# Retention scores and value products as three float32r passes, at later places of a head's pass

## The chip, the cores and the metric

One core of one Trainium2 chip runs the whole kernel. The metric is the device time of one execution in microseconds (us); the median of several runs is compared.

## The reference

The kernel computes one block of a diffusion backbone for 256 latent and 256 context tokens of width 2048 in float32. The latent tokens go through `w_in`, then two attention-like branches of four heads each (retention and gated linear attention, GLA), which are merged by gates, and then a SwiGLU network. What the change touches is the retention branch, for each head:

```python
q_r = apply_rope(to_heads(rq, RET_HEADS), cos, sin) * (RET_DK ** -0.5)
k_r = apply_rope(to_heads(rk, RET_HEADS), cos, sin)
o_r = bidirectional_recurrence(q_r, k_r, v, la_f, la_b, kc, vc, lac_f, lac_b)   # heads of 256 wide
o_r = merge_heads(head_layer_norm(o_r)) * ret_gn * silu(rg)
```

With one decay per head the recurrence is `o = ((q k^T) * decay) v` over 512 keys: 256 of the context, without rope, and 256 latent.

## The kernel before, in words

**Large products.** Every product with a weight matrix is done in float32r, in three passes: the float32 operand is split into a high part (a copy rounded to float32r) and a low part (the value less the high part), and high x high, low x high and high x low are added up in PSUM. A weight slot is 256 rows by 512 columns. SP loads it into `raw` (8 buffers), ScalarE's `split` copies it to `w_hi` (L648), VectorE's `split` subtracts to `w_lo` (L1055), and TensorE's `products` (L1639, L1643, L1651) uses both. `w_hi` and `w_lo` have 4 buffers (`SPLIT`), so ScalarE may split slot p only once TensorE has used slot p - 4 (`w_used`).

**Heads.** The projection `h @ w_in` runs for 15 latent blocks of 8 slots. The heads of both branches are spread over it: one head takes a pass of 16 slots, and `head_pass` calls `at_head(i, p)` behind the slot with number p - 4 of head i's pass, so that the small steps of a head stand between slots on TensorE's queue. ScalarE and VectorE carry out their steps with the same p ahead of their own split of slot p. Each engine's order is written out by hand and each engine takes its queue in order; steps wait for each other by semaphores. Between passes, steps 0 to 3 of the next head stand behind slots 12 to 15.

The steps of a head that matter here, with TensorE's place p before the change:

- p = 3: r_kc transposed into bank 4; ScalarE (p = 4) copies it to `r_kt[:, 0:2]`.
- p = 6: rotated r_q and r_k transposed into banks 5 and 4 (L1907); ScalarE (p = 6) copies them to `r_qt` and `r_kt[:, 2:4]` (L865, L867), then takes the Exp of the far GLA levels (`level_exp`, L834) and only then splits slot 6.
- p = 7: the scores (L1925), fp32, 8 matmuls. VectorE (p = 7, behind its split of slot 6) multiplies the level exponentials (`weigh`, L1268).
- p = 8: the far levels of the GLA (L1891, L1897), which need `weigh`. VectorE (p = 8) weights the scores by the decay into `r_a` (L1329).
- p = 9: the value products (L1941), fp32, 8 matmuls into bank 4.
- p = 10: the GLA values (L1916 to L1919), which need `g_a`. VectorE's `pick_far` (p = 10, behind its split of slot 9) copies bank 6 and parts of `g_near` into `g_a` (L1289, L1294). VectorE then takes the statistics of the retention output (L1337 to L1343), and at p = 11 those of the GLA output.
- p = 13 and 14: the normalised and gated outputs r_g (L1948) and g_g (L1933) transposed; VectorE prepares them at p = 12 and 13 and moves the results to `o_t` at p = 14 and 15.

GpSimd rotates r_q and r_k (`head`, L533 to L537), takes the roots of the variances (L550, L554), and issues the loads of the next head's q, k, v and gates from DRAM (L498). At p of 12 and more, VectorE also takes the near exponents of the next head; at p = 5 the far ones (L1234 to L1237).

## Time and profile before

| | |
|---|---|
| Median of 3 runs | 1721.49 us (1719.5 to 1721.71) |
| The profiled execution's own time | 1720.11 us |
| Its span, first to last instruction | 1718.4 us |
| TensorE busy | 1692.7 us |
| VectorE, ScalarE, GpSimd busy | 1008.8, 740.4, 164.3 us |
| HBM read | 397.99 MB, 244 GB/s over the span with the writes |

The profile is of one execution. A matmul's record includes the time in which its result runs out of the array, so records of a dense stream overlap, and the distance of their starts is what one costs. A fp32 matmul leaves two records, a float32r matmul one. PEld are the weight loads. In the timeline, neighbouring instructions of one kind are merged (xN), and in brackets stands how long the engine idled before, and what released it. Where rows name a line, it is that of the kernel before.

### The profile page before, as it was taken

The page shows a single profiled execution, that of the slowest core. Times are in us where ns is not written, and L with a number is a line of the kernel's source. Part 1 is how long each engine was busy: PE and PEld are TensorE (multiplying, and loading weights), DVE is VectorE, ACT ScalarE, POOL GpSimd, SP SyncE. Part 2 cuts the span into 40 slices and gives each one's busy share as a digit, 9 for nine tenths or more (in the row PEclk, how much of TensorE's full clock was granted, in tenths as well). Part 3 has the DMA queues.
Part 4 walks back from the last instruction along what each step waited for, and adds up shares of the span by engine and source line. Part 5 has one row for each costly group of instructions (what it writes and reads, how often), then busy time and mean ns, then how long its engine had stood idle before and what let it go on. Part 6 is the DMA issues. An engine that isn't in the chain of part 4 may idle for free.

```text
span 1718.4 us, 21875 instructions
## 1 busy us (share of the span) xinstructions
PE 1692.7 (99%) x8109; PEld 1363.7 (79%) x8109; DVE 1008.8 (59%) x1146; ACT 740.4 (43%) x832; POOL 164.3 (10%) x179
## 2 busy tenths in 40 slices
PE   6999999999999999999999999999999999999998
PEld 2458888887878888888888788888888888888886
DVE  2446767748966777666665764454545454444444
ACT  3324222217555454445446654444444444443442
POOL 0011000000046355220000000000000000000000
PEclk9999999999999999999999999999999999999999
DMA  9999999978988666656776566666666666766662
GB/s 366 377 381 372 353 343 363 347 279 304 374 302 275 197 220 197 212 148 222 227 263 218 183 224 192 186 193 185 191 187 189 189 188 189 262 193 193 195 193 90
DMA packets 183676, 419.35 MB, mean 244 GB/s; under 512 B 12960, under 2 KB 13328, under 8 KB 173760
## 3 DMA queue, kind: packets, MB, share of 16 engines
q1 hardware_dynamic: 167680, 375.45, 66.4%
q0 software_dynamic: 7184, 27.71, 4.9%
q10 hardware_dynamic: 8752, 15.38, 2.4%
q8 instruction: 39, 0.64, 0.2%
q14 instruction: 21, 0.17, 0.0%
HBM read 397.99 MB, written 20.50 MB: 244 GB/s over the span
## 4 chain that ended last, share of the span: by engine, by line
PE 96%; DVE 2%; DMA 1%; issue 1%; ACT 0%; POOL 0%; SPq 0%; DVEq 0%; POOLq 0%; ACTq 0%
PE ps L1639 28%; PE ps L1643 28%; PE ps L1651 28%; PE ps L1721 2%; PE ps L1695 2%; DMA raw<-in_w_mod 1%; PE ps L1737 1%; PE ps L1941 1%; PE ps L1925 1%; PE ps L1979 1%; PE ps L1866 0%; PE ps L1684 0%; DVE xr_t L424 0%; PE ps L2057 0%; PE ps L2044 0%
## 5 line engine op out<-in xcount | busy, mean ns | idle before, releaser
L1055 DVE TENSOR_TENSOR w_lo<-raw,w_hi 128x1024 fp32r<-128x1024 f32 x486 | 602.6, 1243 | 501.2 <-ACT w_hi L648 500.9
L648 ACT ACTIVATE w_hi<-raw 128x1024 fp32r<-128x1024 f32 x488 | 515.7, 1060 | 774.0 <-PE ps L1651 758.7
L1639 PE MATMUL ps<-w_hi,h_hi 128*128 128x512 f32 x1440 | 452.6, 395 | 0.0
L1643 PE MATMUL ps<-w_hi,h_lo 128*128 128x512 f32 x1440 | 445.3, 389 | 0.0
L1651 PE MATMUL ps<-w_lo,h_hi 128*128 128x512 f32 x1440 | 392.4, 389 | 0.0
L1643 PEld LDWEIGHTS ps<-w_hi,h_lo 128*128 128x128 f32 x1440 | 270.3, 188 | 56.8
L1651 PEld LDWEIGHTS ps<-w_lo,h_hi 128*128 128x128 f32 x1440 | 270.2, 188 | 56.4
L1639 PEld LDWEIGHTS ps<-w_hi,h_hi 128*128 128x128 f32 x1440 | 266.8, 188 | 55.6 <-ACT w_hi L648 1.5
L1067 DVE SCALAR_TENSOR_TENSOR acc<-wm,csil,acc 128x2048 f32<-128x2048 f32 x60 | 141.0, 2350 | 60.9 <-DMA wm<-in_w_mod 60.8
L1639 PE MATMUL ps<-w_hi,hid_hi 128*128 128x512 f32 x352 | 109.8, 389 | 0.0
L1643 PE MATMUL ps<-w_hi,hid_lo 128*128 128x512 f32 x352 | 109.7, 389 | 0.0
L1651 PE MATMUL ps<-w_lo,hid_hi 128*128 128x512 f32 x352 | 94.7, 389 | 0.0
L1643 PEld LDWEIGHTS ps<-w_hi,hid_lo 128*128 128x128 f32 x352 | 66.1, 188 | 13.8
L1651 PEld LDWEIGHTS ps<-w_lo,hid_hi 128*128 128x128 f32 x352 | 66.1, 188 | 13.7
L1639 PEld LDWEIGHTS ps<-w_hi,hid_hi 128*128 128x128 f32 x352 | 66.0, 188 | 13.7
L1643 PE MATMUL ps<-w_hi,hc_lo 128*128 128x512 f32 x192 | 59.1, 389 | 0.0
L1639 PE MATMUL ps<-w_hi,hc_hi 128*128 128x512 f32 x192 | 59.1, 389 | 0.0
L1651 PE MATMUL ps<-w_lo,hc_hi 128*128 128x512 f32 x192 | 57.8, 389 | 0.0
L1695 PE MATMUL ps<-raw,c_pad 128*32 128x512 f32 x256 | 46.3, 631 | 7.7 <-DMA raw<-in_w_mod 5.8
L628 POOL DMA_DIRECT2D hs<-hsd x1 | 0.7, 718 | 479.2 <-DVE hid_n L1585 479.2
L1117 DVE TENSOR_TENSOR w_lo<-raw,w_hi 128x1024 fp32r<-128x1024 f32 x16 | 19.3, 1223 | 44.5 <-ACT w_hi L721 44.5
L1643 PEld LDWEIGHTS ps<-w_hi,hc_lo 128*128 128x128 f32 x192 | 36.0, 188 | 7.5
(315 smaller groups left out, 1390.5 us busy)
## 6 DMA issues: line engine op xcount, KB each, us to landing
raw<-in_w_in SPq DMA_DIRECT2D x184, 512.0 KB, 6.5
wm<-in_w_mod SPq DMA_DIRECT2D x64, 1024.0 KB, 7.1
raw<-in_ffn_w_gate SPq DMA_DIRECT2D x88, 512.0 KB, 4.4
raw<-in_ffn_w_up SPq DMA_DIRECT2D x88, 512.0 KB, 4.4
raw<-in_ffn_w_down SPq DMA_DIRECT2D x88, 512.0 KB, 4.6
raw<-in_w_mod SPq DMA_DIRECT2D x64, 512.0 KB, 8.1
raw<-in_w_out SPq DMA_DIRECT2D x32, 512.0 KB, 4.8
px<-stage ACTq DMA_DIRECT2D x44, 256.0 KB, 6.1
```

Source lines behind the costliest of these rows:

```text
L648: act.activation(w_hi[:, j % SPLIT, :, :], raw[:, j % RAW, :, :], ACT.Copy).then_inc(w_high, 1)
L1055: dve.tensor_tensor(w_lo[:, j % SPLIT, :, :], raw[:, j % RAW, :, :], w_hi[:, j % SPLIT, :, :].bitcast(F32), ALU.subtract).then_inc(w_low, 1)
L1067: dve.scalar_tensor_tensor(out=a, in0=wm[:, b, :], scalar=csil[:, k:k + 1], in1=a, op0=ALU.mult, op1=ALU.add).then_inc(S("wm_used"), 1)
L1117: dve.tensor_tensor(w_lo[:, o % SPLIT, :, :], raw[:, place % RAW, :, :], w_hi[:, o % SPLIT, :, :].bitcast(F32), ALU.subtract)\
L1639: pe.matmul(o, hi[:, kk, c], w_h[:, e, :], start=kk == 0, stop=False)
L1643: pe.matmul(o, lo[:, kk, c], w_h[:, e, :], start=False, stop=False)
L1651: last = pe.matmul(o, hi[:, kk, c], w_l[:, e, :], start=False, stop=kk == last_k)
L1695: last = pe.matmul(bank(6)[g * GROUP:(g + 1) * GROUP, :], c_pad[:, k, :], raw[:, place % RAW, e, :], start=k < 4, stop=k >= KT - 4, tile_p ...
L1721: last = pe.matmul(bank(n), t[:, 2 * i + e, m * P:(m + 1) * P], w[:, q, e, :], start=i == 0 and r == 0 and a == 0, stop=i == 7 and r == 2 ...
L1737: last = pe.matmul(bank(4 + m), t[:, 2 * i + e, m * P:(m + 1) * P], w[:, q, e, :], start=i == 0 and a == 0, stop=i == 7 and a == 5)
L1925: last = pe.matmul(bank(4, 2)[:, a * L:(a + 1) * L], r_kt[:, 2 * (a // 2) + f, (a % 2) * P:(a % 2 + 1) * P], r_qt[:, f, :], start=f == 0, ...
L1941: last = pe.matmul(bank(4)[:, m * RDK:(m + 1) * RDK], r_a[:, a, m * P:(m + 1) * P], r_v[:, a, :], start=a == 0, stop=a == 3)
```

## The change

- Scores: `r_qt` and `r_kt` become float32r high parts; VectorE makes `r_kt_lo` (context half at p = 4, latent half at p = 7) and `r_qt_lo` (p = 7, ahead of `weigh`). TensorE's scores are 24 float32r matmuls and move from p = 7 to p = 8, ahead of the far levels. The low parts lie in the place of r_q, r_k and r_kc.
- Value products: ScalarE makes `r_v_hi` (p = 7) and `r_a_hi` (p = 10), VectorE `r_v_lo` (p = 8) and `r_a_lo` (p = 10, behind `pick_far`). `r_a` itself moves from p = 8 to p = 9 on VectorE. TensorE's value products are 24 float32r matmuls and move from p = 9 to p = 11. The low part of v lies in v's place, that of a in a's place, `r_a_hi` in the place of the rope's products, `r_v_hi` in that of `ctx_w1`.
- The retention statistics move from VectorE's p = 10 to p = 12; the two branches change places at p = 12 to 15 on VectorE and at p = 13 and 14 on TensorE.
- GpSimd issues the next head's r_kc, r_q and r_k with the v loads, behind `r_o_done` and `g_o_done`; the two roots and the two gate loads change places.

```diff
@@ -179,8 +180,14 @@
 r_v = reg("r_v", [P, 4, RDK], 6)
 r_g = reg("r_g", [P, MT, RDK], 10)
 r_tmp = reg("r_tmp", [P, 4, MT, P], 12)
-r_qt = reg("r_qt", [P, 2, L], 16)
-r_kt = reg("r_kt", [P, 4, L], 18)
+r_qt = reg("r_qt", [P, 2, L], 16, F32R)
+r_kt = reg("r_kt", [P, 4, L], 18, F32R)
+r_qt_lo = reg("r_qt_lo", [P, 2, L], 0, F32R)
+r_kt_lo = reg("r_kt_lo", [P, 4, L], 2, F32R)
+r_v_hi = at("r_v_hi", [P, 4, RDK], F32R, ctx_w1_off)
+r_v_lo = reg("r_v_lo", [P, 4, RDK], 6, F32R)
+r_a_hi = reg("r_a_hi", [P, 4, L], 12, F32R)
+r_a_lo = reg("r_a_lo", [P, 4, L], 22, F32R)
 r_a = reg("r_a", [P, 4, L], 22)
 g_q = reg("g_q", [P, MT, GDK], 26)
 g_k = reg("g_k", [P, MT, GDK], 27)
@@ -542,28 +549,26 @@
         load_g_qk(i + 1)
         pool.wait_ge(S("g_state_done"), i + 1)
         load_g_kw(i + 1)
-        pool.wait_ge(S("r_kc_turned"), i + 1)
-        load_r_kc(i + 1)
-        pool.wait_ge(S("r_qk_turned"), i + 1)
-        load_r_qk(i + 1)
+    pool.wait_ge(S("g_ms_ready"), i + 1)
+    pool.tensor_tensor(hr[:, 1, :, :], mv[:, 1, :, 0:1],
+                       minus_half[:, 0:MT].rearrange("p (m o) -> p m o", o=1), ALU.pow)\
+        .then_inc(S("g_rstd_ready"), 1)
     pool.wait_ge(S("r_var_ready"), i + 1)
     pool.tensor_tensor(hr[:, 0, :, :], mv[:, 0, :, 1:2],
                        minus_half[:, 0:MT].rearrange("p (m o) -> p m o", o=1), ALU.pow)\
         .then_inc(S("r_rstd_ready"), 1)
-    pool.wait_ge(S("g_ms_ready"), i + 1)
-    pool.tensor_tensor(hr[:, 1, :, :], mv[:, 1, :, 0:1],
-                       minus_half[:, 0:MT].rearrange("p (m o) -> p m o", o=1), ALU.pow)\
-        .then_inc(S("g_rstd_ready"), 1)
     if not last:
         pool.wait_ge(S("r_o_done"), i + 1)
         pool.wait_ge(S("g_o_done"), i + 1)
+        load_r_qk(i + 1)
+        load_r_kc(i + 1)
         load_v(i + 1)
-        pool.wait_ge(S("r_on_turned"), i + 1)
-        load_r_gate(i + 1)
         pool.wait_ge(S("g_on_turned"), i + 1)
         pool.wait_ge(stored[0], 16 * 11)
         pool.wait_ge(stored[1], 16 * 11)
         load_g_gate(i + 1)
+        pool.wait_ge(S("r_on_turned"), i + 1)
+        load_r_gate(i + 1)
...
@@ -859,19 +864,24 @@
         if p == 4:
             act.wait_ge(S("r_kc_turned"), i + 1)
             act.activation(r_kt[:, 0:2, :], bank(4).rearrange("p (f n) -> p f n", f=2), ACT.Copy)\
-                .then_inc(S("r_kct_ready"), 1)
+                .then_inc(S("r_high"), 1)
         if p == 6:
             act.wait_ge(S("r_qk_turned"), i + 1)
             act.activation(r_qt[:, :, :], bank(5).rearrange("p (f n) -> p f n", f=2), ACT.Copy,
-                           scale=RDK ** -0.5).then_inc(S("r_qkt_ready"), 1)
+                           scale=RDK ** -0.5).then_inc(S("r_high"), 1)
             act.activation(r_kt[:, 2:4, :], bank(4).rearrange("p (f n) -> p f n", f=2), ACT.Copy)\
-                .then_inc(S("r_qkt_ready"), 1)
+                .then_inc(S("r_high"), 1)
             level_exp(i, 1)
+        if p == 7:
+            act.wait_ge(S("r_v_landed"), i * 32 + 32)
+            act.activation(r_v_hi[:, :, :], r_v[:, :, :], ACT.Copy).then_inc(S("r_high"), 1)
         if p == 9:
             act.wait_ge(S("g_levels_done"), i * 2 + 2)
             act.activation(g_a[:, 2:4, :], bank(7)[:, L:2 * L].rearrange("p (a n) -> p a n", a=2), ACT.Copy)\
                 .then_inc(S("g_cross_ready"), 1)
         if p == 10:
+            act.wait_ge(S("r_a_ready"), i + 1)
+            act.activation(r_a_hi[:, :, :], r_a[:, :, :], ACT.Copy).then_inc(S("r_high"), 1)
             act.wait_ge(S("gates_landed"), i * 32 + 32)
             act.activation(g_g[:, :, :], g_g[:, :, :], ACT.Silu).then_inc(S("g_silu"), 1)
             act.activation(r_g[:, :, :], r_g[:, :, :], ACT.Silu).then_inc(S("r_silu"), 1)
@@ -1322,26 +1332,32 @@
             pick_near(i)
             for e in range(4):
                 exponents(i, 4 + e)
+        if p == 4:
+            dve.wait_ge(S("r_high"), i * 5 + 1)
+            dve.tensor_tensor(r_kt_lo[:, 2:4, :], bank(4).rearrange("p (f n) -> p f n", f=2),
+                              r_kt[:, 0:2, :].bitcast(F32), ALU.subtract).then_inc(S("r_low"), 1)
         if p == 7:
+            dve.wait_ge(S("r_high"), i * 5 + 3)
+            dve.scalar_tensor_tensor(out=r_qt_lo[:, :, :], in0=bank(5).rearrange("p (f n) -> p f n", f=2),
+                                     scalar=RDK ** -0.5, in1=r_qt[:, :, :].bitcast(F32),
+                                     op0=ALU.mult, op1=ALU.subtract).then_inc(S("r_low"), 1)
+            dve.tensor_tensor(r_kt_lo[:, 0:2, :], bank(4).rearrange("p (f n) -> p f n", f=2),
+                              r_kt[:, 2:4, :].bitcast(F32), ALU.subtract).then_inc(S("r_low"), 1)
             weigh(i, 1)
         if p == 8:
+            dve.wait_ge(S("r_high"), i * 5 + 4)
+            dve.tensor_tensor(r_v_lo[:, :, :], r_v[:, :, :], r_v_hi[:, :, :].bitcast(F32), ALU.subtract)\
+                .then_inc(S("r_low"), 1)
+        if p == 9:
             dve.wait_ge(S("r_scores_done"), i + 1)
             dve.tensor_tensor(r_a[:, :, :], bank(4, 2).rearrange("p (a n) -> p a n", a=4),
                               dmat[:, bass.ds(i, 1), :, :].rearrange("p o a n -> p (o a) n"), ALU.mult)\
                 .then_inc(S("r_a_ready"), 1)
         if p == 10:
             pick_far(i)
-
-            dve.wait_ge(S("r_o_done"), i + 1)
...
+            dve.wait_ge(S("r_high"), i * 5 + 5)
+            dve.tensor_tensor(r_a_lo[:, :, :], r_a[:, :, :], r_a_hi[:, :, :].bitcast(F32), ALU.subtract)\
+                .then_inc(S("r_low"), 1)
         if p == 11:
             dve.wait_ge(S("g_o_done"), i + 1)
             for m in range(MT):
@@ -1358,6 +1374,24 @@
                                      in1=mv[:, 1, :, 1:2], op0=ALU.add, op1=ALU.add)\
                 .then_inc(S("g_ms_ready"), 1)
         if p == 12:
+            dve.wait_ge(S("r_o_done"), i + 1)
+            for m in range(MT):
+                dve.bn_stats(stats[:, 0, m, :], bank(4)[:, m * RDK:(m + 1) * RDK]).then_inc(S("r_stat"), 1)
+            dve.wait_ge(S("r_stat"), i * 4 + 2)
+            hold(8)
+            for m in range(MT):
+                dve.bn_aggr(mv[:, 0, m, :], stats[:, 0, m, :]).then_inc(S("r_stat"), 1)
+            dve.wait_ge(S("r_stat"), i * 4 + 4)
+            dve.tensor_scalar(mv[:, 0, :, 1:2], mv[:, 0, :, 1:2], EPS, None, ALU.add)\
+                .then_inc(S("r_var_ready"), 1)
+            dve.wait_ge(S("g_rstd_ready"), i + 1)
+            dve.wait_ge(S("g_silu"), i + 1)
+            for m in range(MT):
+                last = dve.scalar_tensor_tensor(out=g_g[:, m, :], in0=bank(6)[:, m * GDV:(m + 1) * GDV],
+                                                scalar=hr[:, 1, m, :], in1=g_g[:, m, :],
+                                                op0=ALU.mult, op1=ALU.mult)
+            last.then_inc(S("g_on_ready"), 1)
+        if p == 13:
             dve.wait_ge(S("r_silu"), i + 1)
             for m in range(MT):
                 dve.scalar_tensor_tensor(out=r_g[:, m, :], in0=bank(4)[:, m * RDK:(m + 1) * RDK],
@@ -1368,24 +1402,16 @@
             for m in range(MT):
                 last = dve.tensor_scalar(r_g[:, m, :], r_g[:, m, :], hr[:, 0, m, :], None, ALU.mult)
             last.then_inc(S("r_on_ready"), 1)
-        if p == 13:
-            dve.wait_ge(S("g_rstd_ready"), i + 1)
-            dve.wait_ge(S("g_silu"), i + 1)
...
         if p == 14:
+            dve.wait_ge(S("g_on_turned"), i + 1)
+            dve.tensor_tensor(o_t[:, 1, bass.ds(i * 2, 2), :], bank(7).rearrange("p (a n) -> p a n", a=2),
+                              cols[:, bass.ds(i * 2 + 72, 2)].rearrange("p (a o) -> p a o", o=1)
+                              .broadcast_to([P, 2, L]), ALU.mult).then_inc(S("gla_head_done"), 1)
+        if p == 15:
             dve.wait_ge(S("r_on_turned"), i + 1)
             dve.tensor_tensor(o_t[:, 0, bass.ds(i * 2, 2), :], bank(5).rearrange("p (a n) -> p a n", a=2),
                               cols[:, bass.ds(i * 2 + 64, 2)].rearrange("p (a o) -> p a o", o=1)
                               .broadcast_to([P, 2, L]), ALU.mult).then_inc(S("ret_head_done"), 1)
-        if p == 15:
-            dve.wait_ge(S("g_on_turned"), i + 1)
-            dve.tensor_tensor(o_t[:, 1, bass.ds(i * 2, 2), :], bank(7).rearrange("p (a n) -> p a n", a=2),
-                              cols[:, bass.ds(i * 2 + 72, 2)].rearrange("p (a o) -> p a o", o=1)
-                              .broadcast_to([P, 2, L]), ALU.mult).then_inc(S("gla_head_done"), 1)
         if p >= 12 and not final:
             exponents(i + 1, p - 12)
         if p == 15 and not final:
@@ -1885,6 +1911,17 @@
                                      g_arg[:, 0, e, c], start=True, stop=True, tile_position=(0, g * GROUP))
         last.then_inc(S("g_levels_done"), 1)
     if p == 8:
+        pe.wait_ge(S("r_low"), i * 5 + 3)
+        for a in range(4):
+            o = bank(4, 2)[:, a * L:(a + 1) * L]
+            c = slice((a % 2) * P, (a % 2 + 1) * P)
+            for f in range(2):
+                k_hi, k_lo = 2 * (a // 2) + f, 2 * (1 - a // 2) + f
+                pe.matmul(o, r_kt[:, k_hi, c], r_qt[:, f, :], start=f == 0, stop=False)
+                pe.matmul(o, r_kt[:, k_hi, c], r_qt_lo[:, f, :], start=False, stop=False)
+                last = pe.matmul(o, r_kt_lo[:, k_lo, c], r_qt[:, f, :], start=False, stop=f == 1)
+        last.then_inc(S("r_scores_done"), 1)
+    if p == 8:
         pe.wait_ge(S("g_qk_ready"), i * 2 + 2)
         pe.wait_ge(S("g_picked"), i * 9 + 4)
         for m in range(MT):
@@ -1900,7 +1937,7 @@
     if p == 6:
         pe.wait_ge(S("rope_ready"), i * 4 + 4)
         pe.wait_ge(S("ret_head_done"), i + 1)
-        pe.wait_ge(S("r_kct_ready"), i + 1)
+        pe.wait_ge(S("r_low"), i * 5 + 1)
         for b, t in ((5, r_q), (4, r_k)):
             for f in range(2):
                 for m in range(MT):
@@ -1918,30 +1955,24 @@
             pe.matmul(o, g_st[:, 0, c], g_s[:, 0, :], start=False, stop=False)
             last = pe.matmul(o, g_st[:, 1, c], g_s[:, 1, :], start=False, stop=True)
         last.then_inc(S("g_o_done"), 1)
-    if p == 7:
-        pe.wait_ge(S("r_qkt_ready"), i * 2 + 2)
-        for a in range(4):
-            for f in range(2):
-                last = pe.matmul(bank(4, 2)[:, a * L:(a + 1) * L],
-                                 r_kt[:, 2 * (a // 2) + f, (a % 2) * P:(a % 2 + 1) * P], r_qt[:, f, :],
-                                 start=f == 0, stop=f == 1)
-        last.then_inc(S("r_scores_done"), 1)
-    if p == 14:
+    if p == 13:
         pe.wait_ge(S("g_on_ready"), i + 1)
         for f in range(2):
             for m in range(MT):
                 last = pe.transpose(bank(7)[:, f * L + m * P:f * L + (m + 1) * P],
                                     g_g[:, m, f * P:(f + 1) * P], ident[:, :])
         last.then_inc(S("g_on_turned"), 1)
-    if p == 9:
-        pe.wait_ge(S("r_a_ready"), i + 1)
-        pe.wait_ge(S("r_v_landed"), i * 32 + 32)
+    if p == 11:
+        pe.wait_ge(S("r_low"), i * 5 + 5)
         for m in range(MT):
+            o = bank(4)[:, m * RDK:(m + 1) * RDK]
             for a in range(4):
-                last = pe.matmul(bank(4)[:, m * RDK:(m + 1) * RDK], r_a[:, a, m * P:(m + 1) * P],
-                                 r_v[:, a, :], start=a == 0, stop=a == 3)
+                c = slice(m * P, (m + 1) * P)
+                pe.matmul(o, r_a_hi[:, a, c], r_v_hi[:, a, :], start=a == 0, stop=False)
+                pe.matmul(o, r_a_hi[:, a, c], r_v_lo[:, a, :], start=False, stop=False)
+                last = pe.matmul(o, r_a_lo[:, a, c], r_v_hi[:, a, :], start=False, stop=a == 3)
         last.then_inc(S("r_o_done"), 1)
-    if p == 13:
+    if p == 14:
         pe.wait_ge(S("r_on_ready"), i + 1)
         for f in range(2):
             for m in range(MT):
```

The blocks left out are moved without a change to their lines. The definitions of the new tiles stand first.

## Rows read from the trace of the kernel before

**Rows 1.** The page: engines, and the granted clock in 40 slices

```profile
PE 1692.7 (99%) x8109; PEld 1363.7 (79%) x8109; DVE 1008.8 (59%) x1146; ACT 740.4 (43%) x832; POOL 164.3 (10%) x179
...
PEclk9999999999999999999999999999999999999999
```

**Rows 2.** Windows, head passes 2 and 4: us, busy PE, PEld, DVE, ACT, POOL, PEclk, DMA

```profile
607.70:668.60 60.90, 60.90 (x381) 50.82 (x380) 43.73 (x96) 29.59 (x35) 26.55 (x28) 1.00 0.66 204
...
729.50:790.20 60.70, 60.70 (x381) 50.75 (x380) 40.04 (x79) 29.65 (x35) 14.68 (x14) 1.00 0.53 158
```

**Rows 3.** Timeline of TensorE, one pass: start, duration, engine, line, count

```profile
631.34 3.61 PE L1925 MATMUL ps<-r_qt,r_kt 128*128 128x256 f32 x16
...
637.53 0.60 PE L1891 MATMUL ps<-g_arg 128*128 128x128 f32 x4
...
641.69 3.61 PE L1941 MATMUL ps<-r_v,r_a 128*128 128x256 f32 x16
...
647.87 0.59 PE L1916 MATMUL ps<-g_v,g_a 128*128 128x256 f32 x2
...
654.06 0.62 PE L1639 MATMUL ps<-w_hi,h_hi 128*128 128x512 f32 x2
...
656.78 0.62 PE L1639 MATMUL ps<-w_hi,h_hi 128*128 128x512 f32 x2
```

**Rows 4.** Source L1790: float32r matmuls of 256 columns, 64 weight columns

```profile
L1790 PE MATMUL ps<-h_hi,ga_hl x16: 276/276/281, 384.8 to 388.2; 128*64 128x256 f32 x16
```

**Rows 5.** Source L1925, timeline and groups of L1891: loads of 128 columns

```profile
L1925 PEld LDWEIGHTS ps<-r_qt,r_kt x64: 187/190/190, 570.2 to 756.1; 128*128 128x128 f32 x64
...
576.66 0.60 PE L1891 MATMUL ps<-g_arg 128*128 128x128 f32 x4
...
L1891 PE MATMUL ps<-g_arg 128*128 128x128 f32 x16 | 2.4, 273 | 0.0
```

**Rows 6.** Timeline, head 1: ScalarE, then VectorE, around slot 6

```profile
629.77 1.92 ACT L834 ACTIVATE g_arg<-g_arg 128x2048 f32<-128x2048 f32 x1
631.58 2.00 ACT L648 ACTIVATE w_hi<-raw 128x1024 fp32r<-128x1024 f32 x2
...
632.66 1.23 DVE L1055 TENSOR_TENSOR w_lo<-raw,w_hi 128x1024 fp32r<-128x1024 f32 x1 [3.37 <-ACT w_hi L648]
633.80 2.35 DVE L1268 TENSOR_TENSOR g_arg<-g_arg,g_qkt 128x1024 f32<-128x1024 f32 x2
```

**Rows 7.** Timeline, head 0: the same place, with TensorE's scores

```profile
569.46 1.92 ACT L834 ACTIVATE g_arg<-g_arg 128x2048 f32<-128x2048 f32 x1 [0.43 <-DVE g_arg L1237]
...
570.47 3.61 PE L1925 MATMUL ps<-r_qt,r_kt 128*128 128x256 f32 x16
...
572.35 1.23 DVE L1055 TENSOR_TENSOR w_lo<-raw,w_hi 128x1024 fp32r<-128x1024 f32 x1 [1.79 <-ACT w_hi L648]
```

**Rows 8.** Timeline, head 1: slot 5's release to the copies into g_a

```profile
641.88 1.06 ACT L648 ACTIVATE w_hi<-raw 128x1024 fp32r<-128x1024 f32 x1 [2.55 <-PE ps L1651]
...
644.11 0.42 DVE L1289 COPY g_a<-ps 128x256 f32<-128x256 f32 x1
...
644.82 0.75 DVE L1294 COPY_PREDICATED g_a<-mask,g_near 32x64 f32<-32x64 uint8 x3
```

**Rows 9.** Groups by form, VectorE, 548 to 791 us: mean ns of one

```profile
L1375 DVE SCALAR_TENSOR_TENSOR g_g<-ps,hr,g_g 128x256 f32<-128x256 f32 x8 | 3.5, 476 | 0.0
...
L1381 DVE TENSOR_TENSOR o_t<-ps,cols 128x512 f32 x3 | 2.0, 683 | 0.0
```

**Rows 10.** Timeline of GpSimd and TensorE, head 1; DMA issues, 600 to 665 us

```profile
618.10 1.72 POOL L537 TENSOR_TENSOR r_k<-r_tmp 128x256 f32<-128x256 f32 x1
...
630.13 0.72 POOL L498 DMA_DIRECT2D r_k<-px  x1
...
627.73 0.60 PE L1907 MATMUL ps<-ident,r_q 128*128 128x128 f32 x4
...
r_kc<-pc POOLq DMA_DIRECT2D x1, 256.0 KB, 6.5
```

More of the change, by code:

```diff
@@ L114, in build @@
         rope = keep("rope", [P, 2, MT, P])
+        ctx_w1_off = cursor[0]
         ctx_w1 = keep("ctx_w1", [P, GH, L])
@@ L1333, in head @@
                         pick_far(i)
-                        dve.wait_ge(S("r_o_done"), i + 1)
-                        for m in range(MT):
-                            dve.bn_stats(stats[:, 0, m, :], bank(4)[:, m * RDK:(m + 1) * RDK]).then_inc(S("r_stat"), 1)
-                        dve.wait_ge(S("r_stat"), i * 4 + 2)
-                        hold(8)
-                        for m in range(MT):
-                            dve.bn_aggr(mv[:, 0, m, :], stats[:, 0, m, :]).then_inc(S("r_stat"), 1)
-                        dve.wait_ge(S("r_stat"), i * 4 + 4)
-                        dve.tensor_scalar(mv[:, 0, :, 1:2], mv[:, 0, :, 1:2], EPS, None, ALU.add)\
-                            .then_inc(S("r_var_ready"), 1)
+                        dve.wait_ge(S("r_high"), i * 5 + 5)
+                        dve.tensor_tensor(r_a_lo[:, :, :], r_a[:, :, :], r_a_hi[:, :, :].bitcast(F32), ALU.subtract)\
+                            .then_inc(S("r_low"), 1)
                     if p == 11:
@@ L1370, in head @@
                         last.then_inc(S("r_on_ready"), 1)
-                    if p == 13:
-                        dve.wait_ge(S("g_rstd_ready"), i + 1)
-                        dve.wait_ge(S("g_silu"), i + 1)
-                        for m in range(MT):
-                            last = dve.scalar_tensor_tensor(out=g_g[:, m, :], in0=bank(6)[:, m * GDV:(m + 1) * GDV],
-                                                            scalar=hr[:, 1, m, :], in1=g_g[:, m, :],
-                                                            op0=ALU.mult, op1=ALU.mult)
-                        last.then_inc(S("g_on_ready"), 1)
-                    if p == 14:
+                    if p == 14:
+                        dve.wait_ge(S("g_on_turned"), i + 1)
[3 more added lines that the diff above has]
+                    if p == 15:
                         dve.wait_ge(S("r_on_turned"), i + 1)
```

## The prediction

> **What bounds the kernel now.** I read the page first: TensorE is busy in 1692.7 us of a span of 1718.4 us, at the full granted clock in every slice [rows 1]. So a change is worth what it takes off TensorE's queue, less every pause that it puts there. I then cut the trace into the four passes of 16 slots in which the heads run. TensorE is busy in all 60.9 us of each of the four (60.7 in the last), while VectorE has work for 44 us and ScalarE for 30 us [rows 2]: no wait on TensorE's queue ends late in this stretch, and each one has an unknown margin. The margins have to be read from the timelines. One pass on TensorE [rows 3]: a slot of weights without anything behind it takes 656.78 - 654.06 = 2.72 us. The scores begin at 631.34, one slot later the far levels of the GLA begin at 637.53, so the scores take 637.53 - 631.34 - 2.72 = 3.47 us; the value products likewise take 647.87 - 641.69 - 2.72 = 3.46 us.
>
> In what follows s3 means the end of TensorE's slot 3, and so on. Stage p stands on TensorE behind slot p - 4, on ScalarE and VectorE ahead of their split of slot p. ScalarE may split slot p once slot p - 4 is used.
>
> **The matmuls.** Removed: 8 fp32 matmuls for scores and 8 for values in each of four heads. Each shows as two records of 256 columns, 16 records or 3.46 us per block. Added in their place: 24 float32r matmuls of 256 columns per block. The kernel has such passes elsewhere: 32 of them (L1790 and L1791 in turn) run through 384.8 to 388.2 us, 30 gaps between the first and the last start of L1790, so 0.113 us each [rows 4]. Those load only 64 columns of weights, the new ones 128. Does a load of 128 columns fit under a pass of 0.107 to 0.113 us? Its record is 188 ns [rows 5], but four L1891 records with such loads take 0.60 us, of which the last is 0.27 us, so they follow each other at (0.60 - 0.27) / 3 = 0.11 us [rows 5]. I take 0.114 us a pass, 24 x 0.114 = 2.74 us a block. Lower end 24 x 0.107 = 2.6 us, upper end with the load's whole 0.188 us in sight 4.5 us; I stand near the lower end, because the L1891 row has the very load. Saved: 8 x (3.46 - 2.74) = 5.8 us.
>
> The Trainium skill (TensorE: Matmul & The Clock Gate, Part 3, The mechanism) says that LDWEIGHTS overlaps matmuls in flight only when the row group differs, and here all use all rows. The L1891 records don't agree with it at 0.11 us, and by them the sum stands as it is.
>
> **Wait one, the low parts ahead of the scores.** TensorE now needs r_kt_lo and r_qt_lo before the scores. They are moved one slot down to make up for that: they would start at s4 = 631.34 + 2.72 = 634.06. When are the low parts there? ScalarE starts the level Exp at 629.77, the split of slot 6 follows at 631.58, and VectorE can take its own split of slot 6 only at 632.66, after which it is free at 633.80 [rows 6]. Stage 7's new operations stand behind that split: a scalar_tensor_tensor of 128x512 out of PSUM, then a tensor_tensor of 128x512. The tensor_tensor row is 0.683 us; the other kind has 0.476 us for 256 columns, and 256 more cost about (1.23 - 0.683) / 2 = 0.27 us [rows 6, 9], so 0.75 us, of which about 0.09 overlaps with the next one (632.66 + 1.23 against 633.80). The low parts are complete at 633.80 + 0.66 + 0.68 = 635.14. That is 1.08 us after s4; with 0.05 us for the handover and 0.11 us for a first weight load that nothing hides (one step of the L1891 row), TensorE pauses for 1.2 us in heads 1 to 3. The levels need weigh's products, which move to 635.1 + 2.3 = 637.4; the scores end at 635.3 + 2.7 = 638.0, so that is covered.
>
> In head 0 it is worse. There the Exp waits for VectorE's exponents (569.46, 0.43 us of waiting) [rows 7]. The new r_kt_lo of stage 4 stands ahead of them on VectorE and delays them by 0.60 us (0.683 less the overlap); twice that is my upper end, for whatever slows it. Then the split that starts at 572.35 starts at 572.95, the low parts are complete at 572.95 + 1.14 + 1.34 = 575.43, and s4 is at 570.47 + 2.72 = 573.19 [rows 7]: a pause of 2.4 us. In heads 1 to 3 the Exp waits for ScalarE's own two copies, and 0.60 us on VectorE lies under them. Sum of this wait: 2.4 + 3 x 1.2 = 6.0 us.
>
> **Wait two, the GLA values.** L1916 is untouched in the diff, but the value products that stood between slot 5 and slot 6 go to behind slot 7. Its operand g_a comes from pick_far, in stage 10 on VectorE, behind split 9, and split 9 waits for slot 5 to be used. The chain from s5 = 641.69: ScalarE's split 9 starts at 641.88, pick_far at 644.11, and its last copy ends at 644.82 + 0.75 = 645.57 [rows 8], so 3.88 us after s5. So far TensorE had 3.46 + 2.72 = 6.18 us of work there. After the change it has slot 6 alone, 2.72 us. It pauses 3.88 - 2.72 = 1.16 us, with handover and first load 1.3 us, in every head: 5.2 us in all. The extra work on VectorE ahead of it (weigh until 637.4, split 7, r_v_lo and split 8 at 1.14 us each until 640.8, r_a until 642.0) ends before split 9 can start at about 643.7, so it adds nothing.
>
> **The rest costs nothing.** ScalarE's r_v_hi (1.06 us, as the split in [rows 8]) stands ahead of split 7, which TensorE takes 9 us later. r_a_hi follows split 9; r_a_lo is complete some 1.3 us after pick_far, about 5 us before s7, where the values now stand. The statistics and the scaling of g_g (two records of 0.476 us [rows 9] and some short ones, an estimate of 2 us behind the value products) have two slots, 5.4 us, before their transpose; r_g has one more slot. Without these covers each would cost its excess, at most 1 to 2 us a head. GpSimd's queue: r_q, r_k and r_kc are no longer loaded where r_k's issue stands at 630.13, but as the first three of seven loads behind the value products (about 656). Seven issues of 0.72 us take 5 us. The rope still waits for the last gate load, behind the second transpose, so it starts where it did; that transpose is 9 us behind the value products. r_k is ready at 618.10 + 1.72 = 619.8 and needed at 627.73, a cover of 7.9 us; a load took 6.5 us at the most [rows 10]. What is late next if it is exceeded is the transpose of stage 6, and that needs 8 us of delay. SP's queue has no edit and fetches w_in some slots ahead.
>
> **Sum.** -5.8 + 6.0 + 5.2 = +5.4 us against the profiled execution's own 1720.1 us (span 1718.4), so 1725.5 there. The median of the runs shown is 1.4 us above it at 1721.5, so 1726.9 us. Ends of the terms: passes 2.6 us a block -1.1 us; head 0's extra up to +0.6; handovers and first loads between nothing and double, -1.3 to +1.3 us. Own range 1724 to 1730.
>
> **Rivals.** What a measurement of this kernel can tell from no change is about 0.2%, 3.4 us.
>
> 1. Both pauses outweigh the shorter passes, as above: 1726.9, chance 0.62.
> 2. The other side: the low parts and g_a reach TensorE in time, because VectorE's order is not what holds them (ScalarE's split of slots 6 and 9 comes earlier than it did). Then only the passes count: 1721.5 - 5.8 = 1715.7. It is decided by the pauses' sum: below 5.8 - 3.4 = 2.4 us, or 0.3 us each, the kernel is faster. For it speaks that VectorE idles 3.37 us before split 6 [rows 6]; against it that what it idles for is ScalarE, whose order in stages 6 and 9 is the same after. Chance 0.12.
> 3. Only one of the two waits bites: -5.8 + 5.2 or + 6.0, 1721 to 1722. For it: each is an argument of about 1 us on timelines read to 0.1 us. Chance 0.16.
> 4. The weight load isn't hidden under so short a pass: 24 x (0.113 + 0.11) = 5.35 us a block, 8 x (5.35 - 3.46) = +15 us, with the pauses about 1748. Rows 5 speak against it. This is where the skill's sentence above would lead. Chance 0.04.
> 5. A further wait that I see as covered (normalisation, rope) costs 1 us a head more: 1731. Chance 0.06.
>
> The range of 8 in 10 goes from the covered edge of case 3 and part of case 2 to case 5: 1718.5 to 1731. Faster by over 0.2%: 0.13. Within: 0.20, from case 3 and the low edge of case 1. Slower: 0.67.
>
> **What the profile would show.** Right: 24 records a block in about 2.7 us; TensorE idle ahead of the scores, released by r_kt_lo, 2.4 us once and 1.2 us three times; TensorE idle ahead of L1916's successor, released by the copy into g_a, 1.3 us four times; passes of 60.9 + 1.0 us, and the rest of the span unchanged. Wrong: blocks above 3.4 us (case 4), no idle time on TensorE (case 2), or idle time with another releaser (case 5).

## The result

Before: median 1721.16 us over 8 runs (1719.5 to 1721.91). After: 1725.61 us over 8 runs (1725.18 to 1726.83). Ratio 1.0029, 95% interval [1.002, 1.0039]: slower by 4.5 us by the medians, 5.0 us by the ratio. 1726.9 us and +5.4 us were forecast. The profiled execution spans 1723.5 us against 1718.4, +5.1 us, and the heads begin within 0.15 us of each other (first transpose of head 0 at 546.90 us before, 546.75 after), so the difference lies in or behind the heads.

The page after, in the lines of [rows 1]: engines, and the granted clock in 40 slices.

```profile
span 1723.5 us, 22045 instructions
...
PE 1689.2 (98%) x8173; PEld 1361.5 (79%) x8173; DVE 1024.6 (59%) x1166; ACT 747.0 (43%) x840; POOL 164.9 (10%) x179
...
PEclk9999999999999999999999999999999999999999
```

TensorE is busy for 3.5 us less and the span is longer, at the same granted clock in each slice. So TensorE pauses. The waits on its queue in the stretch of the heads (waiting instruction <- what released it: us in all, times, the longest in us):

```profile
PE ps L1953 <- DVE g_a L1304: 4.2, 4, 1.1
PE ps L1920 <- DVE r_kt_lo L1344: 3.9, 4, 1.1
```

Two places, four times each, and no other in the heads. A window of 61.90 us over head 1's pass, against the first row of [rows 2]:

```profile
607.70:669.60 61.90, 59.92 (x397) 50.09 (x396) 48.06 (x100) 31.05 (x37) 26.39 (x28) 1.00 0.65 199
```

TensorE is busy for 59.92 us of it and idle for 1.98 us, where it was busy all the time before. The pass itself, from head 1's first transpose to head 2's, is 671.17 - 609.03 = 62.14 us long instead of 668.63 - 607.76 = 60.87. The timeline of TensorE in that pass, against [rows 3]:

```profile
634.38 1.07 PE L1677 MATMUL ps<-w_lo,h_hi 128*128 128x512 f32 x4
636.37 0.38 PE L1920 MATMUL ps<-r_qt,r_kt 128*128 128x256 f32 x1 [0.92 <-DVE r_kt_lo L1344]
...
639.34 0.61 PE L1928 MATMUL ps<-g_arg 128*128 128x128 f32 x4
...
643.50 0.62 PE L1665 MATMUL ps<-w_hi,h_hi 128*128 128x512 f32 x2
...
645.32 1.07 PE L1677 MATMUL ps<-w_lo,h_hi 128*128 128x512 f32 x4
647.44 0.70 PE L1953 MATMUL ps<-g_v,g_a 128*128 128x256 f32 x2 [1.05 <-DVE g_a L1304]
647.97 0.59 PE L1954 MATMUL ps<-g_v,g_a 128*128 128x256 f32 x2
...
653.76 0.28 PE L1971 MATMUL ps<-r_v_hi,r_a_hi 128*128 128x256 f32 x1
...
656.60 0.62 PE L1665 MATMUL ps<-w_hi,h_hi 128*128 128x512 f32 x2
```

A slot's last row of four L1677 records starts 0.91 us ahead of the slot's end (four steps of 0.2275 us; 642.60 + 0.91 = 643.51 in the complete view, where the next slot's first record stands at 643.50). Slot 4 ends at 634.38 + 0.91 = 635.29 and the scores begin at 636.37: 1.08 us. (The idle time in brackets, 0.92 us here, counts from the end of the last record, 0.16 us behind the slot's end; both figures are used below.) They end at 639.34, 2.97 us for 24 passes, of which 0.11 us is a first weight load with nothing over it. Slot 6 ends at 645.32 + 0.91 = 646.23, and L1953 begins at 647.44: 1.21 us; its second pair stands 0.53 us behind it where 0.43 us is the undisturbed distance, so another 0.10 us. The value products take 656.60 - 653.76 = 2.84 us.

What releases the scores, on ScalarE and VectorE, against [rows 6]:

```profile
631.00 1.92 ACT L839 ACTIVATE g_arg<-g_arg 128x2048 f32<-128x2048 f32 x1
...
632.81 1.06 ACT L653 ACTIVATE w_hi<-raw 128x1024 fp32r<-128x1024 f32 x1
...
633.90 1.22 DVE L1065 TENSOR_TENSOR w_lo<-raw,w_hi 128x1024 fp32r<-128x1024 f32 x1 [2.63 <-ACT w_hi L653]
...
635.04 0.68 DVE L1341 SCALAR_TENSOR_TENSOR r_qt_lo<-ps,r_qt 128x512 fp32r<-128x512 f32 x1
635.64 0.68 DVE L1344 TENSOR_TENSOR r_kt_lo<-ps,r_kt 128x512 fp32r<-128x512 f32 x1
636.24 2.35 DVE L1278 TENSOR_TENSOR g_arg<-g_arg,g_qkt 128x1024 f32<-128x1024 f32 x2
```

From top to bottom this is the chain: Exp, ScalarE's split of slot 6, VectorE's split of slot 6, the two low parts. The last is complete at 635.64 + 0.68 = 636.32, and TensorE starts 0.05 us later. The chain into `g_a`, against [rows 8]:

```profile
643.70 1.06 ACT L653 ACTIVATE w_hi<-raw 128x1024 fp32r<-128x1024 f32 x1 [2.55 <-PE ps L1677]
...
645.94 0.42 DVE L1299 COPY g_a<-ps 128x256 f32<-128x256 f32 x1
...
646.64 0.74 DVE L1304 COPY_PREDICATED g_a<-mask,g_near 32x64 f32<-32x64 uint8 x3
```

From slot 5's end at 643.50 to 646.64 + 0.74 = 647.38 it is 3.88 us, what it was before. The chain has not become slower; what used to stand over it has gone.

### The profile page after: what moved, and what is told of

Its sections match the earlier page's. It is cut to its first block, busy times and chain, and to the rows that moved or that the text cites. A ratio compares the mean times of both kernels' runs of the same rounds, so it can differ in the third digit from the quotient of the medians.

```text
span 1723.5 us, 22045 instructions
## 1 busy us (share of the span) xinstructions
PE 1689.2 (98%) x8173; PEld 1361.5 (79%) x8173; DVE 1024.6 (59%) x1166; ACT 747.0 (43%) x840; POOL 164.9 (10%) x179
## 4 chain that ended last, share of the span: by engine, by line
PE 92%; DVE 3%; issue 2%; DMA 1%; ACT 1%; SPq 0%; POOL 0%; DVEq 0%; ACTq 0%; POOLq 0%
PE ps L1665 27%; PE ps L1669 27%; PE ps L1677 27%; PE ps L1747 2%; PE ps L1721 2%; DMA raw<-in_w_mod 1%; PE ps L1763 1%; PE ps L2010 1%; ACT w_hi L653 1%; ACT g_arg L839 0%; PE ps L1710 0%; DVE xr_t L431 0%; PE ps L1892 0%; DVE w_lo L1065 0%; PE ps L1920 0%
## 5 line engine op out<-in xcount | busy, mean ns | idle before, releaser
L1677 PE MATMUL ps<-w_lo,h_hi 128*128 128x512 f32 x1440 | 392.4, 389 | 0.0
L1677 PEld LDWEIGHTS ps<-w_lo,h_hi 128*128 128x128 f32 x1440 | 270.2, 188 | 56.4
L1677 PE MATMUL ps<-w_lo,hid_hi 128*128 128x512 f32 x352 | 94.7, 389 | 0.0
L1677 PEld LDWEIGHTS ps<-w_lo,hid_hi 128*128 128x128 f32 x352 | 66.1, 188 | 13.8
L1677 PE MATMUL ps<-w_lo,hc_hi 128*128 128x512 f32 x192 | 57.8, 389 | 0.0
L1665 PEld LDWEIGHTS ps<-w_hi,hc_hi 128*128 128x128 f32 x192 | 36.0, 188 | 7.5
```

What stands on the lines that cost most here:

```text
L1665: pe.matmul(o, hi[:, kk, c], w_h[:, e, :], start=kk == 0, stop=False)
L1677: last = pe.matmul(o, hi[:, kk, c], w_l[:, e, :], start=False, stop=kk == last_k)
```

## The experiments

Theory A is the prediction's: two pauses, each a wait for work that VectorE has behind a split, cost more than the shorter passes save. Rivals: only one of the pauses costs time (B); the weight load or the pass itself is the loss (C); the added work on ScalarE and VectorE, not the order, makes the waits (D). All medians below are against the kernel before on the same chip. The lines of these kernels lie up to two off those of after, in `e4_both_fp32_values` and `e5_places_alone` up to 24. The runs are named e1 to e8 for short.

**1. The low parts one stage earlier** (`e1_lows_early`), ahead of VectorE's split of slot 6.

```
-                    if p == 7:
+                    if p == 6:
                         dve.wait_ge(S("r_high"), i * 5 + 3)
...
+                    if p == 7:
                         weigh(i, 1)
```

> The changed kernel with r_qt_lo and r_kt_lo one stage earlier on VectorE, ahead of its split of slot 6 instead of behind it. Theory A (the pause ahead of the scores is the queue: low parts behind split 6, split 6 behind ScalarE's Exp): the low parts are ready before slot 4 ends, the four pauses of 1.08 us with their unhidden first load go, 4 x 1.19 = 4.8 us less than the changed kernel, so +0.3 us against before (ratio 1.000), and the other pause, ahead of the GLA values, stays at about 1.05 us four times. Theory B (VectorE has too much to do in this stretch, or the seven bundled loads slow it): the pause goes elsewhere and the time stays at 1.003.

Measured: ratio 1.0002 [0.9993, 1.0011] (1720.98 against 1720.7 us), span 1718.7 us. TensorE's waits in the heads:

```profile
PE ps L1954 <- DVE g_a L1304: 4.2, 4, 1.1
```

The pause ahead of the scores is gone and the other one is unchanged. The span is 4.8 us shorter than after's: 1.24 + 3 x 1.08 plus the four first loads is 4.9 us.

**2. pick_far one split earlier** (`e2_far_early`), from stage 10 to the end of stage 9, behind `r_a`.

```
+                        pick_far(i)
                     if p == 10:
-                        pick_far(i)
                         dve.wait_ge(S("r_high"), i * 5 + 5)
```

> The changed kernel with pick_far one stage earlier on VectorE, behind r_a and ahead of its split of slot 9. Theory A (the pause ahead of the GLA values is the chain slot 5, ScalarE's split 9, VectorE's split 9, pick_far): g_a is ready about 1.7 us before slot 6 ends, the four pauses with their first load go, 4 x 1.31 = 5.2 us less than the changed kernel, so -0.1 us against before (ratio 1.000), and the pause ahead of the scores stays. Theory B: the time stays at 1.003 or the pause shows on another line.

Measured: ratio 1.0002 [0.9993, 1.0011] (1720.81 us), span 1719.1 us. The waits:

```profile
PE ps L1920 <- DVE r_kt_lo L1344: 3.8, 4, 1.0
```

The other half. Each pause alone cancels the saving, so B is out; with one of them the kernel would have been where the prediction's rival 3 put it.

**3. Both** (`e3_both`).

> The changed kernel with both moves on VectorE. Theory A: no pause is left on TensorE in the heads, and the shorter passes show alone: before - 8 x (3.46 - 2.84) = -5.0 us, a ratio of 0.9971, faster than before. Theory B: not faster than before.

Measured: 1715.99 us (1715.1 to 1719.1, 10 runs), ratio 0.9974 [0.9964, 0.9983], span 1713.6 us. No wait is left on TensorE in the heads. This is faster than both kernels, and rules C out: the products as they stand gain. Head 1 around slot 6:

```profile
628.67 1.92 ACT L839 ACTIVATE g_arg<-g_arg 128x2048 f32<-128x2048 f32 x1
...
629.43 0.68 DVE L1344 TENSOR_TENSOR r_kt_lo<-ps,r_kt 128x512 fp32r<-128x512 f32 x1
...
631.56 1.23 DVE L1065 TENSOR_TENSOR w_lo<-raw,w_hi 128x1024 fp32r<-128x1024 f32 x1 [1.45 <-ACT w_hi L653]
...
632.95 0.28 PE L1921 MATMUL ps<-r_qt,r_kt 128*128 128x256 f32 x1
...
635.83 0.61 PE L1929 MATMUL ps<-g_arg 128*128 128x128 f32 x4
```

`r_kt_lo` is complete at 630.11, 2.8 us ahead of the scores, since it no longer stands behind a split that waits for the Exp. The split isn't delayed by the two operations either: VectorE still idles for 1.45 us ahead of it. The scores of head 0 start at 573.35 and those of head 1 at 632.95, 59.60 us apart, where it was 631.34 - 570.47 = 60.87 before and 636.37 - 574.25 = 62.12 after: -1.27 and +1.25 us a head.

**4. The Exp behind ScalarE's split of slot 6** (`e6_exp_late`). This shortens the same chain at its other end and leaves VectorE's order alone.

```
+                    if p == 7:
                         level_exp(i, 1)
-                    if p == 7:
                         act.wait_ge(S("r_v_landed"), i * 32 + 32)
```

> The changed kernel with ScalarE's Exp of the far levels behind its split of slot 6 instead of ahead of it; VectorE's order is as changed. Theory A: split 6 starts 1.8 us earlier on both engines, so the low parts are ready some 0.7 us before the scores' place: that pause goes (-4.8 us against the changed kernel), and weigh, which needs the Exp, is late by at most a few tenths of a us but is covered by the scores. Ratio 1.000. If the pause hung on VectorE's amount of work alone and not on when split 6 may start, it would stay.

Measured: ratio 1.0007 [0.9998, 1.0016] (1721.98 us), span 1718.7 us, which can't be told from e1, and only the wait for `g_a` is left. Head 1:

```profile
630.68 1.92 ACT L839 ACTIVATE g_arg<-g_arg 128x2048 f32<-128x2048 f32 x1
630.82 1.23 DVE L1065 TENSOR_TENSOR w_lo<-raw,w_hi 128x1024 fp32r<-128x1024 f32 x1 [0.86 <-ACT w_hi L653]
...
632.56 0.68 DVE L1344 TENSOR_TENSOR r_kt_lo<-ps,r_kt 128x512 fp32r<-128x512 f32 x1
...
634.01 0.28 PE L1920 MATMUL ps<-r_qt,r_kt 128*128 128x256 f32 x1
```

The split of slot 6 starts on VectorE beside the Exp, the low parts are there at 632.56 + 0.68 = 633.24, and the scores start at 634.01 without a pause. So the 1.08 us were the Exp ahead of the split, as [rows 6] was read. e1 and e6 keep every operation of the changed kernel and only move some, so for this wait D is out: it is the order and not the amount of work.

**5. e3 with the value products in fp32 again** (`e4_both_fp32_values`), at their new place, without `r_v_hi`, `r_v_lo`, `r_a_hi` and `r_a_lo`.

> The kernel with both moves, but the value products again 8 fp32 matmuls per head at the new place, without the high and low parts of r_a and r_v. Theory A (TensorE's queue alone sets the time, the high and low parts are hidden work): the value blocks go from 2.85 back to 3.45 us, 4 x 0.6 = 2.4 us more than with both moves, ratio about 0.9988, no pause. Rival (the extra work on VectorE and ScalarE costs something of its own): the time comes out below that, down to that of both moves, 0.9974.

Measured: ratio 0.9987 [0.9978, 0.9996] (1718.64 us), span 1716.1 us, no wait. It gives back half of e3's gain, that of four blocks out of eight (1716.1 - 1713.6 = 2.5 us). The four operations that were left out, some 4.5 us a head on ScalarE and VectorE (1.06 + 1.04 + 1.22 + 1.22), cost nothing that can be seen where they stand; the rival's 0.9974 lies just outside the interval.

**6. The places and the loads alone** (`e5_places_alone`): the changed order on all engines, fp32 matmuls, no high or low parts. Of the edit, the scores:

```
-                pe.matmul(o, r_kt[:, k_hi, c], r_qt[:, f, :], start=f == 0, stop=False)
-                pe.matmul(o, r_kt[:, k_hi, c], r_qt_lo[:, f, :], start=False, stop=False)
-                last = pe.matmul(o, r_kt_lo[:, k_lo, c], r_qt[:, f, :], start=False, stop=f == 1)
+                last = pe.matmul(o, r_kt[:, k_hi, c], r_qt[:, f, :], start=f == 0, stop=f == 1)
```

> The changed kernel's places and loads, with fp32 matmuls for scores and values as before and no high or low parts. Theory A: with r_qt and r_kt ready early the scores have no pause, but the GLA values still have theirs, because the value products no longer stand ahead of them: 4 x 1.3 = 5.2 us over before, ratio 1.003, one idle group ahead of the GLA values of about 1.05 us four times. Rival (the pauses come from the low parts' work): no pause and the time of before, 1.000.

Measured: ratio 1.0033 [1.0021, 1.0046] (1726.73 us), span 1724.4 us. The waits:

```profile
PE ps L1929 <- DVE g_a L1299: 4.2, 4, 1.1
```

The wait for `g_a` is there at its full 1.1 us with none of the added work, so it comes from the value products' place and D is out for it. The wait ahead of the scores is not there: without low parts to wait for, the scores begin on time. The span is 6.0 us over that of before, of which 0.7 us is a later start of the heads (547.62 us); the rest fits the 4 x 1.31 = 5.2 us of this wait.

**7. A fourth pass, low x low, in both blocks of e3** (`e7_fourth_pass`). It adds a product of the two low parts that neither kernel computes, 64 passes in all. In the scores:

```
-                last = pe.matmul(o, r_kt_lo[:, k_lo, c], r_qt[:, f, :], start=False, stop=f == 1)
+                pe.matmul(o, r_kt_lo[:, k_lo, c], r_qt[:, f, :], start=False, stop=False)
+                last = pe.matmul(o, r_kt_lo[:, k_lo, c], r_qt_lo[:, f, :], start=False, stop=f == 1)
```

> The kernel with both moves and a fourth pass, low x low, in scores and values: 32 passes a block instead of 24. If one pass with its load of 128 columns costs 0.118 us as its row says, 64 more cost 7.6 us: ratio 0.9974 + 0.0044 = 1.0018. If part of what a block costs is at its edges, less; with a load that isn't hidden (0.188 us) 12 us.

Measured: ratio 1.0018 [1.0009, 1.0027] (1724.11 us), against e3's 0.9974: 0.0044 x 1721.4 = 7.6 us for 64 passes, 0.118 us each. Each of the two ratios is known to 0.0009, so this alone leaves about 0.08 to 0.15 us, and that the third digit fits is luck; a load that isn't hidden, 0.188 us, is outside. The traces say more: the blocks of head 1 take 3.84 and 3.80 us where they take 2.88 and 2.84 in e3, 0.12 us for each added pass. One of the two added groups:

```profile
L1924 PE MATMUL ps<-r_qt_lo,r_kt_lo 128*128 128x256 f32 x32 | 9.1, 283 | 0.0
```

Its mean of 283 ns is the time to a pass's end, in which the next ones already run; it must not be taken for its cost.

**8. One more operation on VectorE ahead of head 0's exponents** (`e8_low_twice`), a second 128x512 subtraction out of PSUM in stage 4 of every head. There is one execution of it, so its time isn't compared.

```
                 dve.wait_ge(S("r_high"), i * 5 + 1)
+                dve.tensor_tensor(r_a[:, 0:2, :], bank(4).rearrange("p (f n) -> p f n", f=2),
+                                  r_kt[:, 0:2, :].bitcast(F32), ALU.subtract)
```

> The changed kernel with one more operation like r_kt_lo (128x512 out of PSUM, into the unused r_a) in stage 4 of every head, 0.60 us more on VectorE ahead of the far exponents. If head 0's Exp starts when VectorE's exponents end, head 0's idle time ahead of the scores grows from 1.1 to 1.7 us; in heads 1 to 3, where ScalarE has 0.9 us in hand, it stays at 0.92. If all four pauses hang on VectorE's amount of work, all four grow by 0.6.

TensorE's first record of the scores in heads 0 and 1, with the idle time ahead:

```profile
577.42 0.38 PE L1922 MATMUL ps<-r_qt,r_kt 128*128 128x256 f32 x1 [1.62 <-DVE r_kt_lo L1346]
...
639.59 0.39 PE L1922 MATMUL ps<-r_qt,r_kt 128*128 128x256 f32 x1 [0.93 <-DVE r_kt_lo L1346]
```

Head 0 pauses 1.62 us instead of 1.08, head 1 0.93 instead of 0.92. So the Exp hangs on VectorE in head 0 and not in head 1, as the prediction read from [rows 6, 7], and after the change head 0 has next to no room left: of 0.60 us, 0.54 arrive. All four idle times together are 4.4 us instead of 3.9, so heads 2 and 3 behave as head 1.

Its span, 1726.8 us, is not to be compared with after's: the heads begin 2.6 us later already (549.35 against 546.75 us). No edit touches the stretch before them, and it differs from execution to execution. The mean granted clock between 20 and 40 us is 0.91 in before and e3, 0.83 in after, and 0.74 in e5, e7 and e8; but the heads of e5 and e7 begin at 547.62 and 547.80 us, so that clock doesn't account for the 2.6 us, and what does stays open. For this reason the verdicts rest on the timed runs. Where whole spans are compared above, the heads begin within 0.2 us of each other (546.87 in e1 and 546.75 in after, 547.09 in e3 and 547.10 in e4, 546.90 in before), or the difference is given.

## Why the prediction was right, point by point

**The bound.** Right: what TensorE's queue does is what the time does, with 1.27 us a head less in e3 and 1.25 us more in after.

**The passes.** 0.114 us was taken and 0.118 to 0.120 measured: 2.84 us for a block of values and 2.86 to 2.88 for one of scores, 2.85 in what follows. The saving is 8 x (3.46 - 2.85) = 4.9 us instead of 5.8. The step "I stand near the lower end" held; the value was that of a bare distance of L1891's 128-column passes, and a 256-column pass with a 128-column load came out some 0.005 us above the 0.113 us of the same pass with 64 columns of weights [rows 4]. Rival 4 is out: these passes all use all rows, and their loads have records of 0.188 us under a step of 0.118 us. The Trainium skill (TensorE: Matmul & The Clock Gate, Part 3, The mechanism) has a sentence by which LDWEIGHTS overlaps only when the row group differs, and the trace doesn't agree with it. The same section also says that a load into the background weight buffer is pulled ahead of matmuls in flight, and a step of 0.118 us would fit that; which buffer a load goes to, no run here shows.

**Wait one, heads 1 to 3.** 1.2 us forecast, 1.08 + 0.11 measured; the low parts were forecast 1.08 us behind slot 4, and stand at 636.32 - 635.29 = 1.03, since the scalar_tensor_tensor took 0.68 us and not 0.75. Shown by e1 and e6 from both ends.

**Wait one, head 0.** The mis-sized term: 2.4 us forecast, 1.24 + 0.11 = 1.35 us measured (slot 4 ends at 573.01 us, the scores begin at 574.25). The step that failed is "The new r_kt_lo of stage 4 stands ahead of them on VectorE and delays them by 0.60 us", added to the 0.43 us by which the Exp already waited. Before and after, first the rows of before:

```profile
549.92 2.83 POOL L533 TENSOR_TENSOR r_tmp<-r_q,rope 128x256 f32<-128x256 f32 x4 [3.13 <-DMA gwd<-gw_rows]
...
552.10 1.74 DVE L1055 TENSOR_TENSOR w_lo<-raw,w_hi 128x1024 fp32r<-128x1024 f32 x1 [2.68 <-ACT w_hi L648]
...
553.76 3.42 DVE L1268 TENSOR_TENSOR g_arg<-g_arg,g_qkt 128x1024 f32<-128x1024 f32 x2
...
561.67 3.44 DVE L1055 TENSOR_TENSOR w_lo<-raw,w_hi 128x1024 fp32r<-128x1024 f32 x2
...
562.32 1.71 POOL L537 TENSOR_TENSOR r_k<-r_tmp 128x256 f32<-128x256 f32 x1
...
565.05 0.22 DVE L1282 COPY_PREDICATED g_near<-mask,ps 128x64 f32<-128x64 uint8 x1
```

```profile
548.82 3.15 POOL L540 TENSOR_TENSOR r_tmp<-r_q,rope 128x256 f32<-128x256 f32 x4 [2.58 <-DMA gwd<-gw_rows]
...
551.95 1.22 DVE L1065 TENSOR_TENSOR w_lo<-raw,w_hi 128x1024 fp32r<-128x1024 f32 x1 [2.68 <-ACT w_hi L653]
...
552.05 1.71 POOL L543 TENSOR_TENSOR r_q<-r_tmp 128x256 f32<-128x256 f32 x1
...
553.09 3.43 DVE L1278 TENSOR_TENSOR g_arg<-g_arg,g_qkt 128x1024 f32<-128x1024 f32 x2
...
560.91 0.80 POOL L543 TENSOR_TENSOR r_k<-r_tmp 128x256 f32<-128x256 f32 x1
...
561.03 1.77 DVE L1065 TENSOR_TENSOR w_lo<-raw,w_hi 128x1024 fp32r<-128x1024 f32 x1
...
561.67 1.73 POOL L544 TENSOR_TENSOR r_k<-r_tmp 128x256 f32<-128x256 f32 x1
...
562.73 0.68 DVE L1337 TENSOR_TENSOR r_kt_lo<-ps,r_kt 128x512 fp32r<-128x512 f32 x1
...
563.33 1.21 DVE L1065 TENSOR_TENSOR w_lo<-raw,w_hi 128x1024 fp32r<-128x1024 f32 x1
...
564.47 0.22 DVE L1292 COPY_PREDICATED g_near<-mask,ps 128x64 f32<-128x64 uint8 x1
...
568.25 0.59 ACT L872 ACTIVATE r_kt<-ps 128x512 fp32r<-128x512 f32 x1
...
568.87 1.92 ACT L839 ACTIVATE g_arg<-g_arg 128x2048 f32<-128x2048 f32 x1
...
574.25 0.38 PE L1920 MATMUL ps<-r_qt,r_kt 128*128 128x256 f32 x1 [1.08 <-DVE r_kt_lo L1344]
```

VectorE's queue has no gap in this stretch, so what it takes there is the Exp's time. From the first of the two splits at 561 to 562 us to the copies behind them it was 565.05 - 561.67 = 3.38 us before and 564.47 - 561.03 = 3.44 us after, with r_kt_lo's 0.60 in between: the new operation cost 0.06. Before, both splits took 1.7 us, beside GpSimd's rope. After, r_kt_lo ran at its 0.68 us under the last of the rope, and the second split started as the rope ended (561.67 + 1.73 = 563.40 us) and took 1.21. The other 0.49 us came from further up: the split at 552.10 took 1.74 us, the one at 551.95 1.22, because the rope's first four steps had ended by then (548.82 + 3.15 = 551.97 us) and its fifth, from 552.05 us on, was the one that came second and took 1.71 us; before, the four steps ran until 549.92 + 2.83 = 552.75. So 0.43 + 0.60 - 0.54 - 0.49 = 0.0: the Exp starts at 568.87, right behind ScalarE's copy, 568.25 + 0.59. That is 1.0 us less than forecast, and the pause is 1.05 us less. Both parts can be seen apart in e5, which has the places and loads but no r_kt_lo. VectorE's splits there:

```profile
552.81 1.23 DVE L1060 TENSOR_TENSOR w_lo<-raw,w_hi 128x1024 fp32r<-128x1024 f32 x1 [2.68 <-ACT w_hi L653]
...
561.90 3.44 DVE L1060 TENSOR_TENSOR w_lo<-raw,w_hi 128x1024 fp32r<-128x1024 f32 x2
```

The first takes 1.23 as in after, the pair 3.44 as before. So the 0.49 us belong to an earlier rope and the 0.54 us to the r_kt_lo under it. The rope's first step starts 19.43 us ahead of ScalarE's copy of r_kt in after, 19.2 to 19.4 us in e1 to e8, and 568.43 - 549.92 = 18.51 us in the one trace of before. It waits for the transfer gwd<-gw_rows, which is issued at 545.70 us in after and 546.25 in before; why it is issued and lands earlier, 0.7 to 0.9 us in all, was not tested. With one trace of before it isn't shown either that this comes from the change: of the two parts of the error, only for the 0.54 us do the runs show a cause in the change.

The Trainium skill says (SBUF — State Buffer, Who interferes with whom) that a VectorE instruction with two inputs in SBUF contends with a GpSimd instruction that reads SBUF, while one with at most one such input does not. These rows agree: the split, with both inputs in SBUF, took 1.74 us where a step of the rope was under way as it began, and r_kt_lo, which has one input in PSUM, took 0.68 us beside the rope as elsewhere.

**Wait two.** 1.16 us and 1.3 with handover and first load forecast, 1.21 and 1.31 measured, four times. Shown by e2, which takes it away, and by e5, which has it alone.

**The rest costs nothing.** Held: the waits view has no third row in the heads, and e4 shows it for the work on the high and low parts of v and a. The roots, the changed places at p = 12 to 15 and GpSimd's loads show no wait either. They were not undone one at a time, but e3 has them all and lies 1713.6 - 1718.4 = -4.8 us against before, which is the passes' saving to 0.1 us.

**The sum.** Forecast -5.8 + 6.0 + 5.2 = +5.4. Measured -4.9 + (1.35 + 3 x 1.19 = 4.9) + 5.2 = +5.2 us against +5.1 in the spans. The two errors, 0.9 us too much saved and 1.1 us too much lost in head 0, cancel; that the sum is right to 0.2 us is luck. In the single head they show: a pass was forecast 1.0 us longer, and head 1's is 1.27 us longer, because its matmuls save 1.2 us and not 1.4. For head 0 the range allowed only for more loss, up to +0.6 us, and the error lies on the other side. With head 0 alone in error the forecast would have been 1 us too high; neither changes the verdict. By the medians the change is +4.5 us (+5.0 by the ratio).

## What to carry over

When a long block leaves the queue of the bounding engine, look at every wait that it stood over: here 3.46 us of value products covered the last 1.2 us of a chain that itself never changed. A new operation whose inputs are there belongs ahead of the queue's next waiting instruction, not behind it; the same two subtractions cost 1.2 us a head behind a split and nothing ahead of it. The version with both moved, e3, runs at 0.9974 of the kernel before.

## What was not expected of the hardware

- Where VectorE's split and GpSimd's rope meet, the one that began second is slowed: splits of 128x1024 took 1.22 us when they began first and 1.74 to 1.77 when they began second, GpSimd's 128x256 steps 0.80 us (the one at 560.91 in after) or 1.73.
- Both pauses on TensorE cost their length plus 0.10 to 0.11 us, the first weight load with no matmul over it.
- The mean granted clock between 20 and 40 us was 0.74, 0.83 or 0.91 in executions of kernels that don't differ there, and the heads began between 546.75 and 549.35 us. The two don't go in step (0.83 with 546.75 in after and with 547.58 in e2), so what moves the start isn't shown.
